# One hybrid decoder layer: sums and spreads of the head norms on array strips, an earlier first weight block, and a reordered stretch of the TensorE schedule

## What is computed

```
n    = rmsnorm(x) * mix_gain ;  proj = n @ w_in
q,k  = rope(rmsnorm per head (64 wide) of the attention projections)
y_att = sparse attention (top 64 keys by a small indexer), 8 heads
y_rwkv = RWKV-7 time mixing, 8 heads, chunks of 64 tokens
         (kk = k*k_k, normalised per head to length 1)
y_mem = cross attention into 256 memory tokens, 4 heads of 128,
         queries and keys rmsnorm'd per head
h = x + (sum over branches of sigmoid(gate) * (y @ w_up)) @ w_out
for each token: 8 heads choose 16 of 16384 experts by product keys
out = h + sum over the 128 chosen of gate * gelu(xn . u_e) * v_e
```

## Time and profile before

| | us |
|---|---|
| runs | 1076.21, 1078.45, 1079.5; median 1078.45 |
| the profiled execution, its own time | 1076.14 |
| its span, first to last instruction | 1074.3 |
| TensorE busy | 839.0 (78%) |
| VectorE busy | 644.8 (60%) |
| ScalarE busy | 391.6 (36%) |
| GpSimd busy | 333.0 (31%) |
| mean TensorE clock granted | 0.873 of full |

### The profile page before, as it was taken

The page is one execution under the profiler, slowest core; times in us unless marked ns, Lnnn a source line. Parts: engine busy times, 40 slices in busy tenths (PEclk is TensorE's granted clock), DMA queues, the critical chain, the costliest instruction groups (busy, mean ns, idle before and its releaser), DMA issues.

```text
span 1074.3 us, 16373 instructions
## 1 busy us (share of the span) xinstructions
PE 839.0 (78%) x5746; PEld 504.4 (47%) x5746; DVE 644.8 (60%) x1567; ACT 391.6 (36%) x1103; POOL 333.0 (31%) x307
## 2 busy tenths in 40 slices
PE   8999999999999999858768667666666556556555
PEld 7888888877888888514223323222111111111111
DVE  3443541187433255867866866876776876876774
ACT  2025133314212112445435435434434434443443
POOL 1000000321011001443454544445454445435441
PEclk9999999999999999988799889778767677677667
DMA  8443333223123275999999999999999999999996
GB/s 324 151 157 118 118 117 107 92 77 119 41 79 120 80 315 239 375 418 426 427 425 427 427 426 426 427 426 427 425 427 426 427 428 427 428 427 423 428 427 274
DMA packets 46874, 329.82 MB, mean 307 GB/s; under 512 B 5344, under 2 KB 5600, under 8 KB 7520
## 3 DMA queue, kind: packets, MB, share of 16 engines
q0 software_dynamic: 36864, 268.45, 59.5%
q1 hardware_dynamic: 8960, 57.77, 14.7%
q10 hardware_dynamic: 992, 2.80, 0.7%
HBM read 327.95 MB, written 1.05 MB: 306 GB/s over the span
## 4 chain that ended last, share of the span: by engine, by line
PE 47%; DMA 20%; DVE 17%; issue 8%; ACT 6%; POOL 1%; POOLq 0%; DVEq 0%; ACTq 0%
DMA pool_mem<-in_experts,pool_mem 19%; PE psum_proj L639 11%; DVE pool_mem L1993 7%; PE psum_proj L1011 7%; PE psum_job L1099 6%; PE psum_proj L1037 4%; PE psum_proj L1074 4%; PE psum_proj L652 3%; PE psum_job L879 2%; DVE pool_mem L1887 2%; DVE pool_mem L1884 1%; POOL pool_mem L2092 1%; PE psum_job L1058 1%; PE psum_proj L1058 1%; ACT L1412 1%
## 5 line engine op out<-in xcount | busy, mean ns | idle before, releaser
L1099 PE MATMUL psum_job<-pool_mem 64*64 64x512 f32 x2048 | 345.1, 780 | 217.2 <-ACT pool_mem L1419 212.3
L2092 POOL DMA_INDIRECT pool_mem<-in_experts,pool_mem x256 | 297.1, 1161 | 411.6 <-PE psum_job L1099 283.5
L1993 DVE CUSTOM_DVE_ANT_0 pool_mem<-pool_mem 128x1024 f32<-128x1024 f32 x256 | 310.1, 1225 | 168.4 <-DMA pool_mem<-in_experts,pool_mem 159.9
L1099 PEld LDWEIGHTS psum_job<-pool_mem 64*64 64x64 f32 x2048 | 84.0, 161 | 460.8 <-issue 459.2
L1412 ACT ACTIVATE pool_mem<-pool_mem 128x1 f32<-128x1 f32 x256 | 51.6, 201 | 269.8 <-DVE pool_mem L1993 250.7
L639 PE MATMUL psum_proj<-pool_mem 128*128 128x256 f32 x544 | 118.8, 379 | 0.7 <-ACT pool_mem L1214 0.7
L639 PEld LDWEIGHTS psum_proj<-pool_mem 128*128 128x128 f32 x544 | 103.1, 190 | 15.4 <-issue 1.6
L1419 ACT ACTIVATE pool_mem<-const,pool_mem 128x64 f32<-128x64 f32 x256 | 89.1, 348 | 18.4
L1416 ACT ACTIVATE pool_mem<-pool_mem 128x1 f32<-128x1 f32 x256 | 75.4, 294 | 9.3
L1011 PE MATMUL psum_proj<-pool_mem 128*128 128x256 f32 x320 | 73.5, 384 | 0.0
L1074 PE MATMUL psum_proj<-pool_mem 128*128 128x256 f32 (+1 forms) x320 | 65.5, 362 | 3.1 <-ACT pool_mem L1444 2.5
(11 more groups left out here) (288 smaller groups left out, 889.2 us busy)
## 6 DMA issues: line engine op xcount, KB each, us to landing
pool_mem<-in_weights SPq DMA_DIRECT2D x50, 1024.0 KB, 4.8
pool_mem<-in_experts,pool_mem POOLq DMA_INDIRECT x256
pool_mem<-in_xT SPq DMA_DIRECT2D x2, 512.0 KB, 5.1
pool_mem<-in_weights ACTq DMA_DIRECT2D x2, 512.0 KB, 9.2
pool_mem<-in_memT SPq DMA_DIRECT2D x1, 1024.0 KB, 12.1
pool_mem<-in_x ACTq DMA_DIRECT2D x1, 1024.0 KB, 13.1
const<-in_const SPq DMA_DIRECT2D x1, 985.5 KB, 15.7
rows<-in_rows SPq DMA_DIRECT2D x1, 512.0 KB, 17.5
```

What stands on the lines that cost most here:

```text
L1099: ins = mm(sum_bank(t, d)[sum_strip(i, d), :], lhsT=diag[rows_, g % DIAGS, :], rhs=slot[g % SLOTS][rows_, D + 512 * d:D + 512 * d + 512], ...
L1993: ins = V.tensor_tensor_reduce(u, u, xn_tok[:, t, :], 1.0, 0.0, ALU.mult, ALU.add, hid[:, par, s_:s_ + 1])
L2092: G_.indirect_dma_start(slot[s_ % SLOTS], None, t_in["experts"], bass.IndirectOffsetOnAxis(ap=expert_i[:, par, s_:s_ + 1], axis=0)).then_i ...
```

## The change

Five edits of one commit.
- **Strips**: a head sum becomes four matmuls of 128 by 32 weights, one for each column strip of 32, without accumulation. A spread becomes four matmuls of 64 rows, so that the two banks are filled from the two row halves in turn; both banks are asked for ahead of the first matmul. The constants shrink by 320 columns, `small` grows by 64, so everything behind them in memory moves by 256 columns (1 KB).
- **Start**: `vec` is issued by SP behind the first half of x; ScalarE's queue begins with weight block 0. 13 matmuls of ones instead of 11.
- **Copies**: ScalarE copies mem_v between the sigmoids of `wl` and those of `al`.
- **Schedule**: half a gate unit goes in front of `value 0`; `pair 1`, the gate halves, `rhs 0` and `y 0` around it move as shown.
- **Transposes** of the last output block come one quarter of a query unit earlier.

```diff
-for _name, _n in [("ident", 128), ("headsel", 2), ("pick_pairs", 128), ("pick_ones", 224), ("rot", 128), ("causal", 128),
+for _name, _n in [("ident", 128), ("headsel", 2), ("pick_pairs", 32), ("rot", 128), ("causal", 128),
...
-CONST["pick_pairs"] = (CONST["pick_pairs"][0], 224)
...
-    out["pick_pairs"] = np.zeros((P, 128))
-    out["pick_pairs"][:, 96:128] = p[:, None] // HD == np.arange(32)[None, :] // 16
-    out["pick_ones"] = np.zeros((P, 224))
-    out["pick_ones"][:, 96:128] = 1.0
+    out["pick_pairs"] = p[:, None] // HD == np.arange(32)[None, :] // 16
...
-    ("invA", 0, 4), ("pair", 0), ("value", 0), ("invX", 0, 4), ("gate", 0), ("exp", 2),
-    ("invA", 0, 5), ("pair", 1), ("value", 1), ("invX", 0, 5), ("exp", 3), ("gate", 1),
-    ("rhs", 0), ("pair", 2), ("gate", 0), ("value", 2), ("u", 0), ("y", 0), ("gate", 1),
+    ("invA", 0, 4), ("pair", 0), ("gate", 0), ("value", 0), ("invX", 0, 4), ("pair", 1), ("exp", 2),
+    ("invA", 0, 5), ("gate", 1), ("value", 1), ("invX", 0, 5), ("exp", 3),
+    ("pair", 2), ("gate", 0), ("rhs", 0), ("value", 2), ("gate", 1), ("u", 0), ("y", 0),
     ("rhs", 1), ("pair", 3), ("gate", 0), ("value", 3), ("u", 1), ("y", 1), ("gate", 1),
...
-        small = sb("small", [P, 208])
+        small = sb("small", [P, 272])
...
                 sp.dma_start(in_sq["x"][:, 4 * j:4 * j + 4, :].rearrange("p a b -> p (a b)"),
                              t_in["xT"][:, 1024 * j:1024 * j + 1024]).then_inc(x_in[j], 16)
+                if j == 0:
+                    sp.dma_start(vec[:, :], t_in["vec"]).then_inc(vec_in, 16)
...
-                    w = n // CT
-                    pick = c("pick_ones" if w == 1 else "pick_pairs")
+                    pick = ones[:, 0:32] if n == CT else c("pick_pairs")
                     for k in range(CT):
-                        first = 96 - 32 * k
-                        ins = mm(o, lhsT=pick[:, first:first + P], rhs=sq[:, k, :], start=(k == 0), stop=(k == CT - 1))
+                        ins = mm(o[32 * k:32 * k + 32, :], lhsT=pick, rhs=sq[:, k, :], start=True, stop=True)
                 end(ins, (x + "_ss",))
...
-                for i, job in enumerate(spread_jobs(x)):
-                    o = halves(begin(job))
-                    for m in range(2):
-                        k = 2 * i + m
-                        to_chunk = ident[:, 32 * k:32 * k + 1].to_broadcast([P, P]) if w == 1 else \
-                            c("to_heads")[:, k * P:(k + 1) * P]
-                        ins = mm(o[:, m, :], lhsT=to_chunk, rhs=stat[x], start=True, stop=True)
-                    end(ins, job)
+                o = [halves(begin(job)) for job in spread_jobs(x)]
+                for m in range(2):
+                    for i, job in enumerate(spread_jobs(x)):
+                        k, r = 2 * i + m, slice(64 * i, 64 * i + 64)
+                        to_chunk = ident[r, 32 * k:32 * k + 1].to_broadcast([64, P]) if n == CT else \
+                            c("to_heads")[r, k * P:(k + 1) * P]
+                        ins = mm(o[i][:, m, :], lhsT=to_chunk, rhs=stat[x][r, :], start=True, stop=True)
+                        if m == 1:
+                            end(ins, job)
...
-            for _ in range(11):
+            for _ in range(13):
...
-                if i == 2:
+                if i == 1:
                     out_transposes(3)
...
-                act.dma_start(vec[:, :], t_in["vec"]).then_inc(vec_in, 16)
...
+            def copy_mem_v():
+                for i in range(2):
+                    wait_unit(act, "mem_v", i)
+                    unit_read(nc.scalar.copy(vm[:, :, 256 * i:256 * i + 256], halves(ubank("mem_v", i))), "mem_v", i)
...
             for j, b, dst in (("wl", "w0", sgw), ("al", "a0", a_gate)):
+                if j == "al":
+                    copy_mem_v()
...
-            for i in range(2):
-                wait_unit(act, "mem_v", i)
-                unit_read(nc.scalar.copy(vm[:, :, 256 * i:256 * i + 256], halves(ubank("mem_v", i))), "mem_v", i)
```

## The result

| | before | after |
|---|---|---|
| median of four runs each, us | 1077.74 | 1064.83 (1062.03 to 1065.02) |
| ratio, 95% interval | | 0.9879 [0.9867, 0.989] |
| the profiled execution, its own time | 1076.14 | 1064.74 |
| its span | 1074.3 | 1062.9 |
| first gather | 423.27 | 412.53 |

A forecast was written before the change was run, and what follows sets the result against it. TensorE's front was taken to set the first gather, with transfer-bound gathers behind it. Terms 4.0 + 2.5 + 1.3 + 1.5 + 1.1 + 2.0 + 0.1 = 12.5 us off the 1078.45 median gave near 1066, range 1062.5 to 1072.

The forecast's parts named there:

- The frame: Whole kernel: gathers are bound by transfers and untouched; a microsecond TensorE's path loses ahead of 423 moves the end one for one.
- The fourth rival: Gathers: the new memory layout slows them; at 3% slower pace the kernel takes 1085 us; chance 0.04.
- The first: Rival at the start: vector lands at 11 or later, the start gives nothing; 8.5 us gained in all, 1070; chance 0.15.
- the third: Rival: covers fail in several places (start, strips or order), gain within 3.2 us, 1076 to 1078; chance 0.07.
- The start: Kernel start, up to units 1 and 2: earlier landings and full clock save 4.0 us (ends 0 and 4.3).
- the wall: At the start: unit 2 needs unit 0's bank, free only near 20.8 us, which limits the saving of 4.1 to 4.0.
- Strips and halves: Head sums and spreads: 0.65 us per sum, saving 1.08; two spread pairs in 1.07 instead of 1.73, saving 0.66.
- The second rival: Head sums: column strips run one after another, sums cost 1.9 us, gain 7.9, so 1070.5; chance 0.12.
- mem_q 0: Mk sum, mem_v copies, kn sum: this unit starts at 92.25 instead of 94.78, saving 2.5 us, ScalarE still last.
- idx_q: Kn spread and mq sum, ahead of this unit: 0.25 of the spread's saving arrives, the sum adds 1.08; 1.3 us.
- Spreads of q and k: Ahead of the rotations: k sum and both spreads save 1.08 + 0.66 + 0.66 us that turn into idle time, gaining 0.
- The order: Schedule around value 0: half a gate unit fills TensorE's 2.07 us wait, less 0.25 lost; saves 2.0 us (ends 0 and 2.3).

The follow-up runs named there:

- after_warm11: The changed kernel with 11 warm-up matmuls instead of 13; ratio to the kernel before 0.9888 [0.9871, 0.9905].
- strips_only: The kernel before with only the sums on column strips and the spreads in row halves; ratio 0.9976 [0.9964, 0.9989].
- after_vec_back: The changed kernel with the parameter vector again first in ScalarE's queue, 13 warm-up matmuls kept; ratio to the kernel before 0.9936 [0.9919, 0.9953].
- after_fill: The changed kernel with two added matmuls, their result unread, ahead of each of the spreads of q and k; ratio to the kernel before 0.988 [0.9862, 0.9898].
- start_only: The kernel before with only the vector behind the first half of x and 13 warm-up matmuls; ratio 0.9973 [0.9961, 0.9984].
- the four parts alone: The kernel before with one part each: strips and halves 0.9976, start 0.9973, schedule order 0.9976, copies of mem_v 0.9994 (ratios).
- before_again: The kernel before, unchanged, run once more for a second profile; one run, 1076.62 us, first gather at 424.13.

## Why the prediction was right, and where not

**The frame held.** TensorE's front sets the first gather, and the gathers take what they took: 651.0 us from the first one to the end before, 650.4 after. The fourth rival, the memory layout, is out: the pace is 426 GB/s. The first is out, since the vector landed at 6.49 and not at 11, and so is the third, since the gain is four times its 3.2 us.

**The start gave 3.25 instead of 4.0, and not by my working.** The landings were near (first halves 5.2 to 5.6 forecast, 6.0 and 6.2 found; the vector 7.2 and 6.49; x's second half 8.7 and 8.87), and the folds ended at 13.09, 13.1 forecast. But I had unit 0 "end near 11.4", 3.5 us behind its start: it has 32 records of 0.216, 6.9 us, so I had counted half of them. The same working with 6.9 puts unit 1 at 15.2 and the start's gain at 2.7. That 3.25 came out is due to the vector, which landed 0.7 earlier than forecast. With the right length unit 0 is the chain, the sum of x waits for it and not for the folds (14.24), and the wall that I bounded the start with, unit 0's bank at 20.8, never comes into play. That error hid what the clock does: of 3.25, only 1.54 is the earlier start, and 1.7 is unit 0 at full clock. In the profile of after_warm11 that part is gone with two warm-up matmuls.

**Strips and halves** cost what the nearest rows said: 0.57 from start to start with the change of tile shape (0.65 taken), 1.06 (1.07 taken). The second rival is out: four strips that share all rows took 0.61 us together, where one alone has 0.43 of moving data. The Trainium skill, "TensorE: Matmul & The Clock Gate", Part 3, says that weight loads overlap running matmuls only where the row group differs. The trace does not agree: the eight weight loads of a sum lie within 0.19 us from 104.18, while its matmuls run from 104.21. The Trainium skill, "TensorEngine Tiling (Array Packing)", "Key Properties", says that a change of the tiling mode drains the engine. Here it stayed at the 0.1 taken: the unit ahead of the mk and mq spreads, 13.90 before from its start to theirs, takes 13.99.

**mem_q 0** came as worked out, 2.59 for 2.5, and with ScalarE last. **idx_q** gained 1.50 for 1.3: ScalarE's reading of mem_q 1 ended 1.1 behind the unit, as the spread did, and the wait was 0.16 where I had reckoned with 0.4.

**Spreads of q and k.** "The 1.08 + 0.66 + 0.66 there turn into idle time": that was right, 3.2 us of it. The step that failed is the silent one behind it, that idle time off the critical path costs nothing. In the profiled execution the low clock made the rotation 1.58 us longer, and the stretch as a whole lost 1.37 where I had put 0. The other profiles bear on the cause. Four executions had all three gaps (the changed kernel, strips_only, after_vec_back, after_warm11), and three of them ran the rotation slowly; of the ten with at most one gap longer than 0.3 us there, none did. after_fill alone keeps the order, the narrow spreads and the last gap of 0.80, and has the full clock. So the gaps are very likely the cause, and it is no cost of every execution: how often it falls due in the runs without a profile is open. I had read the same effect at the start and did not carry it to the gaps that the change itself would open.

**The order** gave 2.29 for 2.0; the wait for the state was 0.29 for 0.25. Where the other 0.3 come from I did not trace.

**Sum.** 12.5 forecast, 10.7 in the front of the profiled pair: -0.75 for the start, -1.37 for the spreads of q and k, +0.36 for the rest. The whole of the profiled pair differs by 11.4, with the 0.7 behind the first gather. That the medians differ by 12.9 is because the kernel before was profiled in an execution 1.6 below its median (1076.14 and 1077.74), and the changed kernel in one at its median (1064.74 and 1064.83). What made those 1.6 is not shown. The clock can do it: the second profile's start was 0.9 worse, and start_only lost 1.5 behind the wait ahead of value 0, though only one execution in six did. The gathers can do it too: over all the profiles the time behind the first gather reaches from 649.3 to 651.7. So the agreement with 12.4 is part luck: the front gave 1.8 less than forecast, and the 0.7 behind the first gather and the 1.6 of the profiled execution's place, neither of which is a term of the sum, made up for it.

## What to carry to other kernels

When a change shortens TensorE's work in a place where another engine is last, look at the gap that it opens and put independent work into it, or leave the work wide: a narrower form won nothing there, and in three of four profiled executions with the gaps the rotation behind them was 1.3 to 1.6 us slower. Count what a wait costs with the clock behind it, and judge edits one by one only beside the kernel they will live in: the four parts alone add to 0.8%, together they gave 1.2%, with intervals of 0.1% each way on every one of these ratios. Of that difference 0.6 us is the two waits that hide one another; the rest is not traced, though low clocks behind waits that the other parts remove took 1.7 us of strips_only and 1.5 of start_only. Look also at what stands at the head of a queue: 43 KB in rows of 344 bytes there made the 512 KB behind them land 7.5 us after their issue (7.7 in after_vec_back), and 5.4 without them. Whether the short rows or only the place does it was not tried apart.

## What the runs showed that I had not expected

The length of a gap does not tell whether TensorE's clock falls to the 1.2 GHz level behind it. Ahead of unit 0, gaps of 2.03 to 3.47 us were followed by a slow unit 0 in all eight executions that had one (8.59 to 9.93 us), and gaps of 0.71 to 1.37 in none of six (7.14 to 7.15). But the gap of 2.07 ahead of value 0 was followed by the low clock in one execution of six, and the gap of 1.98 ahead of mem_q 0 in the one that had it (strips_only). The three gaps of 1.16, 1.26 and 0.80 were in three of four: after_warm11 has them to 0.01 as the changed kernel does, and its rotation took 1.96. The same gaps can thus cost nothing or 1.5 us from one execution to the next.

And in before_again unit 0's 32 records took 9.46 us where 6.9 is full pace, while the clock's row reads full speed:

```profile
9.06 9.46 PE L700 MATMUL psum_proj<-pool_mem 128*128 128x256 f32 x32 [2.99 <-DMA pool_mem<-in_weights]
```
```profile
12.00:13.00 1.00, 1.00 (x3) 0.80 (x3) 0.00 (x0) 0.00 (x0) 0.00 (x0) 1.00 0.97 410
```

Three records begun or running in that microsecond, as in the earlier trace rows with four at 0.50, so I read the pace of the records, and not the clock's row alone.
